# Moving four projection pieces and the split of the mixed rows to later attention steps

## What is computed

```
for l in range(DEPTH):                                  # DEPTH = 2
    h = _rmsnorm(x, norm1_g[l])
    q, k, v, su, sv, cb, cc, cx = jnp.split(h @ w_in[l], split_at, axis=-1)
    q = _axial_rope(_rmsnorm(q, q_norm_g[l]), tabs)
    k = _axial_rope(_rmsnorm(k, k_norm_g[l]), tabs)
    a_out = _block_attention(q, k, v)                   # 8 heads, 512 x 512 scores
    g_out = _spatial_gating(su, sv, sg_norm_g[l], sg_w[l], sg_b[l])
    c_out = cb * _dwconv3(cc * cx, conv_w[l])
    mix = jnp.concatenate([a_out, g_out, c_out], axis=-1)
    x = x + mix @ w_out[l]
    up = _dwconv3(_rmsnorm(x, norm2_g[l]) @ ffn_w_up[l], ffn_conv_w[l])
    gate, val = jnp.split(up, 2, axis=-1)
    x = x + (jax.nn.silu(gate) * val) @ ffn_w_down[l]
```

## Time and profile before

| | us |
|---|---|
| median of 3 runs | 3502.27 |
| lowest and highest | 3502.13, 3506.35 |
| the profiled execution | 3499.91 |
| its span in the trace | 3498.3 |
| TensorE busy in the span | 3045.6 |
| VectorE, ScalarE, GpSimd busy | 1128.4, 1103.0, 954.0 |

### The profile page before, as it was taken

How to read it: one execution, slowest core, us unless ns; L and a number is a source line. 1 busy time by engine, 2 the same in 40 slices (tenths; PEclk the granted TensorE clock), 3 DMA queues, 4 the chain that set the end, 5 groups by cost and what they waited for, 6 DMA issues and landing times. The chain is left out here.

```text
span 3498.3 us, 43658 instructions
## 1 busy us (share of the span) xinstructions
PE 3045.6 (87%) x15079; PEld 2023.0 (58%) x15079; DVE 1128.4 (32%) x2067; ACT 1103.0 (32%) x1803; POOL 954.0 (27%) x886
## 2 busy tenths in 40 slices
PE   7998987887886898989787887598999989899999
PEld 5775675333333676667333333365788766578877
DVE  4355343111111446434211111334443322534330
ACT  4424332222221523432222222234333323433331
POOL 3411230111111331132111111421444443134543
PEclk7999998999997999999899999799999999999999
DMA  6214426999998212434899999511222331123232
GB/s 222 73 59 150 150 67 240 408 408 409 408 406 299 97 59 79 165 120 150 325 408 408 410 408 407 190 55 49 73 97 73 100 114 55 49 69 98 74 83 74
DMA packets 289713, 663.69 MB, mean 190 GB/s; under 512 B 20191, under 2 KB 114709, under 8 KB 289553
## 3 DMA queue, kind: packets, MB, share of 16 engines
q1 hardware_dynamic: 271680, 623.43, 47.8%
q0 software_dynamic: 17872, 38.14, 3.0%
HBM read 653.64 MB, written 25.69 MB: 194 GB/s over the span
## 5 line engine op out<-in xcount | busy, mean ns | idle before, releaser
L894 PE MATMUL psum<-s_parts 128*128 128x512 f32 (+1 forms) x4000 | 1014.2, 405 | 70.1 <-ACT s_units L2353 16.4
L894 PEld LDWEIGHTS psum<-s_parts 128*128 128x128 f32 (+1 forms) x4000 | 765.4, 193 | 279.0 <-issue 40.6
L894 PE MATMUL psum<-s_ring,s_units 128*64 128x512 f32 x3168 | 743.4, 618 | 139.1 <-DMA s_ring<-in_w_expert_in 96.4
L872 POOL TENSOR_TENSOR s_parts<-s_ring,s_parts 128x512 fp32r<-128x512 f32 x368 | 471.3, 1317 | 753.5 <-ACT s_parts L2181 753.5
L894 PEld LDWEIGHTS psum<-s_ring,s_units 128*64 128x64 f32 x3168 | 246.5, 141 | 592.6 <-issue 451.7
L894 PE MATMUL psum<-s_h_low,s_parts 128*128 128x512 f32 (+1 forms) x2000 | 499.9, 391 | 8.5 <-DVE s_h_low L1624 6.8
L782 POOL TENSOR_TENSOR s_parts<-s_ring,s_parts 128x512 fp32r<-128x512 f32 (+1 forms) x210 | 268.2, 1314 | 677.1 <-ACT s_parts L2181 677.1
L894 PEld LDWEIGHTS psum<-s_h_low,s_parts 128*128 128x128 f32 (+1 forms) x2000 | 373.1, 187 | 98.6 <-issue 9.1
L2181 ACT ACTIVATE s_parts<-s_ring 128x4096 fp32r<-128x4096 f32 (+3 forms) x80 | 259.3, 3241 | 193.7 <-PE psum L894 112.5
L894 PE MATMUL psum<-s_units 128*128 (+9 forms) x1520 | 275.3, 394 | 51.6 <-DVE s_gsl L1880 21.8
L820 POOL DMA_INDIRECT s_units<-h_scratch,s_take_at x66 | 78.7, 1193 | 610.2 <-DVE s_take_at L1874 474.7
(11 more groups left out here) (375 smaller groups left out, 2644.2 us busy)
## 6 DMA issues: line engine op xcount, KB each, us to landing
s_ring<-in_w_expert_in SPq DMA_DIRECT2D x132, 2048.0 KB
s_ring<-in_w_expert_out SPq DMA_DIRECT2D x66, 2048.0 KB
s_ring<-in_w_in SPq DMA_DIRECT2D x28, 2048.0 KB, 8.7
s_ring<-in_w_ada SPq DMA_DIRECT2D x24, 2048.0 KB, 8.6
s_ring<-in_ffn_w_up SPq DMA_DIRECT2D x40, 1024.0 KB, 6.6
s_ring<-in_ffn_w_down SPq DMA_DIRECT2D x16, 1408.0 KB, 7.1
s_ring<-in_w_out SPq DMA_DIRECT2D x8, 2048.0 KB, 8.1
s_units<-ys_scratch POOLq DMA_DIRECT2D x16, 512.0 KB, 7.4
```

Of the source, the lines that this page charges most:

```text
L872: ins = pool.tensor_tensor(parts[:, s, cols], ring[:, s, cols], parts[:, 4 + n % 2, cols].bitcast(F32), ALU.subtract)
L894: return pe.matmul(o, lhsT=lhsT, rhs=rhs, start=start, stop=stop)
```

## The change

Two tables and one condition are changed, for both layers of the second kind. The two pieces of each of the two `cb` products move two steps back: from steps 10 and 11 to 12 and 13, and from 12 and 13 to 14 and 15. The product with `cb` moves from step 14 to 16. The parts of the mixed rows, before behind steps 14 to 18, now stand behind 16 to 18, four rows of them behind 16.

```
-... 10: (("cb", 0), 0, 2), 11: (("cb", 0), 2, 3),
-        12: (("cb", 1), 0, 2), 13: (("cb", 1), 2, 3)}
+... 12: (("cb", 0), 0, 2), 13: (("cb", 0), 2, 3),
+        14: (("cb", 1), 0, 2), 15: (("cb", 1), 2, 3)}
...
-MIX_SPLIT = {14: (0, 1), 15: (4, 5), 16: (6, 7), 17: (2,), 18: (3,)}
+MIX_SPLIT = {16: (0, 1, 4, 5), 17: (6, 7, 2), 18: (3,)}
...
-                if j == 14:
+                if j == 16:
                     for x in range(2):
                         ve.wait_ge(TB.by(("cb", x)).sem, TB.freed_at(l, ("cb", x)))
                         ve.tensor_tensor(cb[:, x, :], T[:, x, :], cb[:, x, :], ALU.mult).then_inc(convolved.sem, convolved.more())
```

More of the change, by code:

```diff
@@ L226 @@
 FILL = {0: (("cc", 0), 0, 3), 1: (("cx", 0), 0, 3), 2: (("sv", 0), 0, 2), 3: (("sv", 0), 2, 3), 4: (("sv", 1), 0, 2), 5: (("sv", 1), 2, 3),
-        6: (("cc", 1), 0, 2), 7: (("cc", 1), 2, 3), 8: (("cx", 1), 0, 2), 9: (("cx", 1), 2, 3), 10: (("cb", 0), 0, 2), 11: (("cb", 0), 2, 3),
-        12: (("cb", 1), 0, 2), 13: (("cb", 1), 2, 3)}
+        6: (("cc", 1), 0, 2), 7: (("cc", 1), 2, 3), 8: (("cx", 1), 0, 2), 9: (("cx", 1), 2, 3), 12: (("cb", 0), 0, 2), 13: (("cb", 0), 2, 3),
+        14: (("cb", 1), 0, 2), 15: (("cb", 1), 2, 3)}
 BESIDE = {3: ("ws",), 7: ("svt", 0), 8: ("svt", 1), 12: ("mix", 0), 13: ("mix", 1)}
```

## The result

Over 20 executions of each, taken in turn, the changed kernel has a median of 3512.57 us (3505.95 to 3527.52) and the kernel before 3506.14 us (3502.03 to 3517.92). The ratio is 1.0023 with a 95% interval of 1.0013 to 1.0032, that is 8.1 us slower, 4.6 to 11.2; the two medians differ by 6.4 us. A second series later gave 1.0026 (1.0015 to 1.0037), with medians 7.1 us apart. One execution of the kernel before, in the series beside e5 to e8, took 3692.74 us at a granted clock of 0.806 where the others have 0.93 to 0.94, and the ratios leave it out. The forecast had the changed kernel 6.1 us slower, which I took for less than a measurement could tell, and 3508.4 us as its time, in a range up to 3511.8. The effect is as forecast in kind and near it in size; the time lies above the range.

The account below looks back on a forecast made before the run. TensorE's waits in the last two layers' attention, chiefly 4.84 us before T14, were taken as the bound. pv3 1.50 us later plus 1.55 us longer made 3.05 us a layer, 6.1 in all, on 3502.27: 3508.4 us, range 3502.3 to 3511.8.

Parts of the forecast that it names:

- T14: Transposes of step 14: wait of 2.4 us instead of 4.84, start 0.74 us earlier, run at the lower clock.
- Steps 10 to 13: Stretch that the first cb pieces leave or enter: 3.78 us earlier at step 10, 4.05 us earlier by pv2.
- T11: Transposes of step 11: a new wait of 1.9 us for a ScalarE copy, until 2408.81 us.
- pv2: Third product with the values, after the exponentials of step 13: at 2413.51 us, 4.05 us earlier.
- the first rival: Slower by more than 0.2%: lower clock in more steps, also at T11; 3509.4 to 3513.6 us, chance 0.22.
- Step 14 and 15: Second cb product: 3.78 us before T12 and 1.98 us more before T13, spending the early gain almost whole.
- T12: Transposes of step 12, behind 16 cb matmuls: at 2420.87 us, 0.27 us earlier.
- T13: Transposes of step 13, behind the last 8 cb matmuls: at 2427.80 us, against 2426.09 before.
- the second rival: Clock falls once, not at T14: pv3 0.66 us later and slow, 2.21 us a layer, 3506.7 us, chance 0.12.
- pv3: Fourth product with the values: 1.50 us later behind VectorE's low parts, then 5.20 us long at low clock, +1.55 us.
- The rule: Skill's claim that PSUM copies keep TensorE warm: no wait here would lower the clock, giving 3503.6 us.
- The cover: First feed-forward block's load, issued 13.6 us later, costs nothing: needed only behind 23 us of projection.

Follow-up runs that it names:

- e5: Changed kernel with VectorE's second convolution behind the gating of step 13 instead of step 11; ratio to the kernel before 1.0003.
- e8: e7 with the two products with cb also behind the copy of step 15's transposes; ratio to the kernel before 0.9972.
- e2: Kernel before with only the products with cb and the mixed rows' parts moved to step 16, pieces where they were; ratio to the kernel before 1.0015.
- e11: Kernel before again, unedited, a single execution; stage 55.27 and 54.69 us in the two layers, no ratio.
- e7: Changed kernel with the edits of e1, e5 and e6 together; ratio to the kernel before 0.9960.
- e10: Changed kernel again, unedited, for a second trace; ratio to the kernel before 1.0026.
- e9: Changed kernel with matmuls of no use, three in the wait before T14 and five before pv3; ratio to the kernel before 1.0004.
- e1: Changed kernel with the high and low parts of all step 16 rows moved to step 17, behind the copy of step 15's transposes; ratio to the kernel before 0.9997.
- e6: Changed kernel with the last 8 matmuls of cb before T14 (step 16) instead of T13 (step 15); ratio to the kernel before 0.9993.

## Why the prediction was right in its mechanism and missed its number

**What bounded the kernel** was read rightly: T14's wait hung on VectorE's products and low parts in step 14. e2, which takes these away alone, cuts it by 2.0 us. My list of TensorE's waits left out 1.54 us in front of the piece of step 12 and 0.70 us before rb3; nothing in the sum hung on them.

**Steps 10 to 13.** Right. From pv1, T11 stands at 21.46 us (21.41 forecast) with a wait of 1.87 us (1.9), and pv2 at 26.45 (26.11). The third of a microsecond more isn't the clock, as pv2 stands at 26.45 in the second layer too; VectorE's gating product beside GpSimd's work took 1.59 us and not the 1.25 us of the trace before. The clock did fall around T11 in the first layer, as the first rival feared: the matmuls of the gating and L14 took 3.77 us for 20 instructions, and pv2's wait shrank from 1.81 us (second layer, where they took 2.15) to 0.19. So the fall cost nothing at all, not 0.5 us: the wait behind it was there to take it up. Nor is 1.77 us of waiting a bound under which the clock holds, as I had it from two rows: behind that wait it fell in e11 and in the second layer of e7.

**Step 14 and 15.** T12 at 33.80 us (33.47) and T13 at 40.65 us (40.40) from pv1. The piece in front of T12 spent the gain as worked out.

**T14.** Its wait was 2.33 us against 2.4 forecast. I had the clock low under it; it was at the full level under T14 in all four layers traced, and fell under T15 in two of them. So VectorE's copy of T14 started 1.12 us behind T14, not 2.00, and pv3 came 50.10 us after pv1, 0.77 us later than before, not 1.50: the row that I took (a wait of 2.12 us lowered the clock at once) was one instance, and the fall can also come a microsecond later. So this term was 0.73 us a layer too high, and the second rival had it right (0.66 us).

**pv3.** The order on VectorE made it late, by six operations of 0.60 us, exactly as put. The low clock cost 1.54 us in the better layers (5.19 against 5.20 taken) and up to 2.84 (6.49) in the worse, within the ends given. That 5.20 was met so closely is chance: behind a long wait the same 16 matmuls took anything from 4.98 us (e2) to 6.49 us (e10). It is luck too that the two errors nearly cancel in the sum of two layers: 2.30 and 3.35 us a layer in the first trace, 3.61 and 2.30 in the second, 5.65 and 5.91 us for two layers, against 6.1.

**The number.** The step that failed is the last one of the sum, its base, and with it the range. I added the effect to a median of three executions, 3502.27 us, and drew the range from the other terms alone. Over 20 executions the same kernel has 3506.14 us: the base was 3.9 us too low. The measured 3512.57 us is 4.2 us above my 3508.4; 3.9 of this is the base and 0.3 the effect (the medians differ by 6.4 us, and I had 6.1). The range ended only 3.4 us above the forecast, so the base alone carried the time out of it; 3.9 us higher, from 3506.2 to 3515.7 us, it would have held. The table of times showed the scatter, 3502.13 to 3506.35 in three; the base needed a term in the range like any other. Of the effect itself, 6.1 us forecast, 5.65 and 5.9 traced, the medians have 6.4 and 7.1 us and the ratio 8.1 us (4.6 to 11.2) and 9.1 (5.3 to 13.0): the traces lie within both intervals, low. The 2 to 3 us between traces and ratio are within the noise and aren't found in a place: outside the stage the two traces don't differ that way (from the second projection to the end 431.7 us before and 430.4 after). It stays open whether the mean execution has more low clock than those profiled. I gave "within 0.2%" 0.74, and the result is on the slower side of it: my forecast lay only 0.9 us under that bound, and so close to a bound the chances on either side are near even.

**The rule.** The Trainium skill, TensorE: Matmul & The Clock Gate, section "Loop structure matters more than you think", says that copying a result out of PSUM doesn't break the array's warmth. I took it for a rule on every wait that ends with such a copy, and this the trace refutes: pv3 behind 3.48 us of waiting for one took 5.19 us at a granted clock of 0.73, and with the waits filled (e9) 3.65 at 1.00. But the section's example has the next matmuls follow immediately, and here TensorE stood still until the copy was done; so no run here speaks against the example as it stands, only against my use of it.

**The cover** held: the later load of the feed-forward block (the DMA share is 1.08 in 2434 to 2437 us) delayed nothing that the trace shows.

## What to carry to other kernels

Filling an engine's idle steps with work taken from earlier steps wins only if the earlier steps get shorter for everyone: here VectorE's unbroken run kept the early gain to 3.8 us, and a piece of 3.8 us in front of the next exponentials spent it. On an engine that works strictly in order, put work that nobody waits for yet behind the copy that frees a bank, not in front of it: two products and four low parts of 0.6 us each in front of T15's copy made the change a loss, and with the four low parts behind it (e1) the loss was gone by the ratio. It took e5 and e6 as well to make it a gain. Treat the clock as a term that belongs to a group of waits: removing one of the three long waits bought back some 4 us of stage, removing all three 16.3, more than the sum. And when a forecast is a time, give the base a term of its own: three executions had their median 3.9 us under that of twenty.

## What the runs showed of the hardware

Two things I had not expected. First, some of VectorE's operations are much longer while GpSimd works, above all those with two inputs in SBUF. The same step of the convolution, first in the changed kernel at step 11, then in e7 at step 13, and below them GpSimd's work in the same two kernels:

```profile
2403.40 1.67 DVE L2134 SCALAR_TENSOR_TENSOR s_temps<-s_units,s_par,s_temps 128x511 f32<-128x511 f32 x1
```

```profile
2413.22 0.75 DVE L2134 SCALAR_TENSOR_TENSOR s_temps<-s_units,s_par,s_temps 128x511 f32<-128x511 f32 x1
```

```profile
2400.53 11.05 POOL L872 TENSOR_TENSOR s_parts<-s_ring,s_parts 128x512 fp32r<-128x512 f32 x8 [63.38 <-ACT s_parts L2181]
```

```profile
2400.32 10.43 POOL L872 TENSOR_TENSOR s_parts<-s_ring,s_parts 128x512 fp32r<-128x512 f32 x8 [65.13 <-ACT s_parts L2181]
```

The operation of 1.67 us lies inside GpSimd's 11.05 us, that of 0.75 us begins 2.5 us behind the end of GpSimd's 10.43. Even an operation of two columns, the negated maxima that the exponentials wait for, took 1.23 us in e7 and 0.16 us where GpSimd is idle:

```profile
2409.54 1.23 DVE L2087 SCALAR_TENSOR_TENSOR s_lamv<-s_lamv 128x2 f32<-128x2 f32 x1
...
2416.14 0.16 DVE L2087 SCALAR_TENSOR_TENSOR s_lamv<-s_lamv 128x2 f32<-128x2 f32 x1
```

The Trainium skill, SBUF — State Buffer, section "Who interferes with whom", says that a VectorE instruction with two SBUF inputs contends with a GpSimd instruction that reads SBUF; the trace agrees, with these numbers. What reads only PSUM kept its time beside GpSimd: the maxima of the logits took 1.22 us there and elsewhere, the copy of T 0.68 us. The product that opens the convolution (line 2133), with one row of SBUF as input, took 1.00 us beside GpSimd and 0.48 alone. So the later place has two effects: the convolution leaves the path, and it shrinks from 4.5 us in the changed kernel (2402.36 to 2406.86 us) to 2.2 us in e5 and e7 (2412.71 to 2414.88 us in e7). In return the negated maxima of step 13 come while GpSimd still works, and cost e5 the microsecond that it missed.

Second, the clock under the same instructions isn't the same from layer to layer. In one execution (e10) the wait before T14 was 2.33 us in both layers, and yet T15 took 1.83 us in the first and 1.19 in the second, and pv3 6.49 and 5.19 us. What decides where the clock falls, no run here shows.
